# Hybrid stick-breaking and HGRN2 layer: the HGRN2 output projection in pairs of panels by seven products

## What is computed

```
h    = rmsnorm(x, norm_g);  proj = h @ w_in          # 10240 columns
sb_q, sb_k, sb_v, sb_z, hg_q, hg_f, hg_i, hg_z, gate_logits = split(proj)
sb_o = stick_breaking_attention(sb_q, sb_k, sb_v)     # 8 heads of 128
u_sb = (sb_o * silu(sb_z)) @ w_sb_proj                # 1024 x 1024
hg_o = rmsnorm(hgrn2(silu(hg_q), 1 - f, log f, hg_i)) # 8 heads of 128
u_hg = (hg_o * silu(hg_z)) @ w_hg_proj                # 1024 x 1024
y    = sigmoid(gate_sb) * u_sb + sigmoid(gate_hg) * u_hg
out  = rmsnorm(x + y @ w_out, final_norm_g)
```

## Time and profile before

| | |
|---|---|
| median of 3 timed runs | 1359.74 us (1359.3 to 1360.8) |
| the profiled execution | 1358.94 us, its span 1357.2 us |
| mean granted clock of TensorE | 0.997 of full |
| PE busy | 1329.0 us (98%) |
| DVE, ACT, POOL busy | 903.1, 549.4, 709.5 us |
| sb and hg panels on PE | 1087 to 1263 us |
| output product on PE | 1263 to 1351 us |

### The profile page before, as it was taken

The page is one execution under the profiler, slowest core; times in us unless marked ns, Lnnn a source line. Parts: engine busy times, 40 slices in busy tenths (PEclk is TensorE's granted clock), DMA queues, the critical chain, the costliest instruction groups (busy, mean ns, idle before and its releaser), DMA issues.

```text
span 1357.2 us, 22985 instructions
## 1 busy us (share of the span) xinstructions
PE 1329.0 (98%) x8393; PEld 1108.9 (82%) x8393; DVE 903.1 (67%) x1076; ACT 549.4 (40%) x899; POOL 709.5 (52%) x475
## 2 busy tenths in 40 slices
PE   8899999999999999999999999999999999999998
PEld 6788788788878878878888887887887888888886
DVE  5838877877877887787687788778635455645223
ACT  7543355255345335524534533552444431111121
POOL 5655564654665556455466556645578722223310
PEclk9999999999999999999999999999999999999999
DMA  5122111211112211121111211113543485434502
GB/s 187 31 62 65 47 62 32 82 58 46 62 46 73 66 32 62 31 92 56 37 62 46 77 62 31 62 31 118 176 180 133 155 266 191 124 93 132 202 27 98
DMA packets 128168, 118.55 MB, mean 87 GB/s; under 512 B 3920, under 2 KB 110464, under 8 KB 128128
## 3 DMA queue, kind: packets, MB, share of 16 engines
q1 hardware_dynamic: 118816, 92.81, 21.5%
q10 hardware_dynamic: 9312, 25.19, 5.4%
HBM read 88.63 MB, written 29.36 MB: 87 GB/s over the span
## 4 chain that ended last, share of the span: by engine, by line
PE 82%; DVE 7%; issue 5%; POOL 2%; ACT 2%; DMA 1%; ACTq 0%; DVEq 0%; SPq 0%; POOLq 0%
PE banks L1693 44%; PE banks L1986 13%; PE banks L2030 7%; PE banks L1773 5%; PE banks L1751 4%; PE banks L1763 2%; DVE hk L1176 2%; DVE forget L1176 2%; DVE scT L1422 1%; PE banks L1832 1%; PE banks L1737 1%; PE banks L1807 1%; POOL b_lo L631 1%; POOL b_sum L631 1%; PE banks L1834 1%
## 5 line engine op out<-in xcount | busy, mean ns | idle before, releaser
L1693 PE MATMUL banks<-a_hi,b_hi 128*128 128x512 f32 x1064 | 432.7, 407 | 6.4 <-issue 3.8
L1693 PE MATMUL banks<-a_hi,b_lo 128*128 128x512 f32 x1064 | 417.1, 392 | 0.0
L1693 PE MATMUL banks<-a_lo,b_hi 128*128 128x512 f32 x1064 | 415.7, 391 | 0.0
L631 POOL TENSOR_TENSOR b_lo<-w_raw,b_hi 128x512 fp32r<-128x512 f32 x106 | 162.2, 1540 | 231.9 <-ACT b_hi L733 231.9
L631 POOL TENSOR_TENSOR b_lo<-b_sum,b_hi 128x512 fp32r<-128x512 f32 x114 | 167.7, 1471 | 148.2 <-ACT b_hi L733 148.2
L1693 PEld LDWEIGHTS banks<-a_hi,b_hi 128*128 128x128 f32 x1064 | 200.3, 188 | 46.1 <-issue 7.5
L1693 PEld LDWEIGHTS banks<-a_hi,b_lo 128*128 128x128 f32 x1064 | 199.9, 188 | 44.3
L1693 PEld LDWEIGHTS banks<-a_lo,b_hi 128*128 128x128 f32 x1064 | 200.8, 189 | 35.9
L733 ACT ACTIVATE b_hi<-b_sum 128x512 fp32r<-128x512 f32 x114 | 72.0, 632 | 152.5 <-POOL b_sum L631 151.9
L717 POOL TENSOR_TENSOR w_lo<-w_raw,w_hi 128x1024 fp32r<-128x1024 f32 x20 | 54.5, 2730 | 133.5 <-ACT w_hi L733 133.5
L631 POOL TENSOR_TENSOR b_sum<-w_raw 128x512 f32<-128x512 f32 x68 | 102.9, 1513 | 0.0
(11 more groups left out here) (219 smaller groups left out, 2564.8 us busy)
## 6 DMA issues: line engine op xcount, KB each, us to landing
w_raw<-in_w_in SPq DMA_DIRECT2D x72, 512.0 KB, 4.9
gate_d<-gate_out SPq DMA_DIRECT2D x16, 512.0 KB, 4.6
gate_in<-gate_d ACTq DMA_DIRECT2D x32, 256.0 KB, 2.7
x_tok<-in_x SPq DMA_DIRECT2D x8, 512.0 KB, 6.6
z_d<-z_out SPq DMA_DIRECT2D x8, 512.0 KB, 2.7
hz_d<-z_out SPq DMA_DIRECT2D x8, 512.0 KB, 2.7
osb_d<-o_sb SPq DMA_DIRECT2D x8, 512.0 KB, 5.7
ohg_d<-hq SPq DMA_DIRECT2D x8, 512.0 KB, 2.7
```

Of the source, the lines that this page charges most:

```text
L631: return nc.gpsimd.tensor_tensor(dst, a, b, op)
L1693: last = mm(bank, w[:, s, k, :], t[s][:, k, :], start=opens and k == 0 and z == 0, stop=k == QUAD - 1 and z == 2, skip_group_check=not opens)
```

## The change

1. **hg's branch** is made of four pairs by seven products, 12 matmuls each, like the input projection: 336 matmuls for 384. Its weights go through `hg_prepare` (POOL), `hg_split` (ACT) and buffers of their own; only `w_raw` holds raw weights, no second buffer.
2. **The hg operand** is now needed as seven block sums. DVE gates two tiles per sb panel (`gate_ohg`), makes four sums of 2048 elements a partition (`branch_sums`) in panels 5 and 6, and seven low parts (`branch_low`) from panel 6 into the first pair; ACT makes seven high parts of 2048 (`branch_high`).
3. **y's first share** (gated u_sb) is stored to memory by SP (`store_y`) and read back (`load_y`). DVE takes a block in PSUM: add, times gate, plus y's share (`y_part`), ACT makes the high part (`y_high`), DVE the low part (`y_low`).
4. **The output's weights**: panels 0 and 1 are loaded when the last pair's raw weights are free, 2 and 3 behind them, 4 to 7 after the last product.
5. **`HG_AT`**: the pieces from level 6 on come one half product later.
6. **s_ready**: at pair 2 PE waits product by product (P6 and P7 for two operands, P5 for three, P3 for four); ACT's second sigmoid of head 0 waits for all four.
7. In the gate pairs with two or more sb tiles DVE takes c22 ahead of the second `osb_gate`; their low parts come later.

```diff
-HG_AT = {1: 0, 3: 1, 6: 3, 9: 4, 12: 5, 14: 6, 17: 7, 19: 8, 21: 9, 23: 11, 26: 12}
+HG_AT = {1: 0, 3: 1, 6: 3, 9: 4, 12: 5, 15: 6, 18: 7, 20: 8, 22: 9, 24: 11, 27: 12}
+Y_BLOCKS = ((1, 1), (0, 0), (1, 0), (0, 1))
...
+        def hg_freed(engine, n, s):
+            if n > N_PAIRS:
+                engine.wait_ge(product_done, products_before(n - 1, s))
+            elif s in (P5, P2):
+                engine.wait_ge(panel_done, 2 * KT - 2)
+            elif s in (P3, P4):
+                engine.wait_ge(panel_done, 2 * KT)
...
 def load_panel(t, source, first):
+                elif OUT_PANEL0 <= t < OUT_PANEL0 + 2:
+                    sp.wait_ge(raw_sum, 4 * (N_PAIRS + N_HG_PAIRS))
                 else:
                     sp.wait_ge(panel_ready, t - 1)
...
+            def load_hg_pair(n):
+                if n == N_PAIRS:
+                    sp.wait_ge(panel_ready, KT)
+                else:
+                    sp.wait_ge(raw_sum, 4 * n)
+            def load_gate(i):
+                if i < 2:
+                    sp.wait_ge(gated, 2 * KT)
+                else:
+                    sp.wait_ge(y_made, i - 1)
...
+            for i in range(N_HG_PAIRS):
+                if i < N_HG_PAIRS - 1:
+                    load_hg_pair(N_PAIRS + i + 1)
+                else:
+                    load_panel(out_panel(0), w_out[0], 0)
+                    load_panel(out_panel(1), w_out[0], P)
+                    load_y(KT - 1)
+                    load_panel(out_panel(2), w_out[0], 2 * P)
+                    load_panel(out_panel(3), w_out[0], 3 * P)
+                if i == 0:
+                    for e in range(2, KT - 1):
+                        load_y(e)
+                for j in range(4 * i + 2, min(4 * i + 6, 4 * N_HG_PAIRS)):
+                    load_gate(j)
...
+            for i in range(N_HG_PAIRS):                       # DVE
+                n = N_PAIRS + i
+                dve.wait_ge(p1_copied, n + 1)
+                take(n, 0, P6 + 1, hg_u2[:, :], pair_bank(n, P6), hg_u3[:, :])
+                if i == 0:
+                    branch_low(P4)
+                else:
+                    y_low(4 * i - 1)
+                take(n, 1, P7 + 1, hg_u3[:, :], pair_bank(n, P7), hg_u2[:, :])
+                y_part(4 * i, P5, hg_u3)
+                y_part(4 * i + 1, P2, None)
+                y_low(4 * i)
+                y_part(4 * i + 2, P3, hg_u2)
+                y_low(4 * i + 1)
+                y_part(4 * i + 3, P4, hg_u2)
+                y_low(4 * i + 2)
...
 PE:
+                    if isinstance(n, int) and n == 2 and s in SUM_OPERANDS:
+                        pe.wait_ge(s_ready, max(SUM_OPERANDS.index(t) for t in SUM_OPERANDS if t <= s) + 1)
-            pe.wait_ge(s_ready, 4)
             second_half(0)
...
             pe.wait_ge(y_ready, 2 * KT - 1)
+            pe.wait_ge(panel_ready, OUT_PANEL0 + 2)
             for g in range(2):
-                out_group(g, 2, 2)
+                out_group(g, 0, 2)
```

More of the change, by code:

```diff
@@ L389, in build @@
         gated = sem("gated")
-        y_part = sem("y_part")
+        y_stored = [sem("y_stored0"), sem("y_stored1")]
+        y_back = [sem(f"y_back{e}") for e in range(KT)]
+        block_gated = sem("block_gated")
+        y_made = sem("y_made")
         y_hi_ready = sem("y_hi_ready")
@@ L586, in _ @@
+            sp.wait_ge(product_done, PRODUCTS * (N_PAIRS + N_HG_PAIRS))
+            for i in range(NT):
+                sp.dma_start(x_again[i][:, :], x[0, i * P:(i + 1) * P, :]).then_inc(x_again_in, 16)
+            sp.dma_start(fg[:, :], final_g.rearrange("(a n) -> a n", a=1).broadcast_to([P, D])).then_inc(fg_in, 16)
+            for e in range(4, KT):
+                load_panel(out_panel(e), w_out[0], e * P)
             for done, (i, cols) in enumerate(NORM_PIECES):
                 sp.wait_ge(normed, done + 1)
-                sp.dma_start(out[0, i * P:(i + 1) * P, cols], res[:, i, cols]).then_inc(stored, 16)
+                sp.dma_start(out[0, i * P:(i + 1) * P, cols], res[i][:, cols]).then_inc(stored, 16)
@@ L917, in sigmoids @@
                 act.wait_ge(qk_done, 8 * h + j + 1)
+                if isinstance(h, int) and h == 0 and j == 1:
+                    act.wait_ge(s_ready, 4)
                 bank, n_banks, m = score_banks(j)
@@ L1102, in _ @@
                             osb_sigmoid(e)
-                    if p == 7 and not final:
-                        for e in OSB_GATED.get(g, ()):
+                    if p in (7, 10) and not final:
+                        for e in OSB_GATED.get(g, ())[:1] if p == 7 else OSB_GATED.get(g, ())[1:]:
                             osb_high(e)
@@ new lines, in _ @@
+                if t == KT - 2:
+                    for s in (P1, P6, P7):
+                        branch_high(s)
+                if t < KT - 1:
+                    fetch_gate(t + 1)
+            hg_split(N_PAIRS, P1)
+            hg_split(N_PAIRS, P7)
+            branch_high(P5)
+            hg_split(N_PAIRS, P6)
+            hg_split(N_PAIRS, P5)
+            branch_high(P2)
+            hg_split(N_PAIRS, P2)
+            branch_high(P3)
+            for i in range(N_HG_PAIRS):
+                n = N_PAIRS + i
+                last_pair = i == N_HG_PAIRS - 1
+                for p in range(PAIR_POINTS):
+                    if i == 0 and p == 0:
+                        hg_split(n, P3)
+                    if p == 1:
+                        hg_split(n, P4)
+                        act.wait_ge(product_done, PRODUCTS * n + P1 + 1)
+                        act.wait_ge(block_taken, 5 * n - 2)
+                        copy(hg_u3[:, :], pair_bank(n, P1)).then_inc(p1_copied, 1)
+                    if i == 0 and p == 2:
+                        branch_high(P4)
+                    if i > 0 and p == 2:
+                        y_high(4 * i - 1)
+                    following = {6: P1, 7: P7, 9: P6, 10: P5, 11: P2, 12: P3}
+                    if p in following and not last_pair:
+                        hg_split(n + 1, following[p])
+                    if last_pair and p in (4, 5, 8, 12):
+                        e = (4, 5, 8, 12).index(p)
+                        act.wait_ge(product_done, PRODUCTS * n + (P6 if e < 2 else P7) + 1)
+                        split_panel(out_panel(e), out_weights(e)[0])
+                    if p in (10, 11, 13):
+                        y_high(4 * i + (10, 11, 13).index(p))
@@ L1158, in _ @@
+            y_high(4 * N_HG_PAIRS - 1)
+            act.wait_ge(product_done, PRODUCTS * (N_PAIRS + N_HG_PAIRS))
+            for e in range(4, KT):
+                split_panel(out_panel(e), out_weights(e)[0])
             for i in range(NT):
@@ L1654, in _ @@
+            y_low(4 * N_HG_PAIRS - 1)
             dve.wait_ge(x_again_in, 16 * NT)
[L1655 removed]
             def last_norm(i):
```

405 lines of the change are left out of this document (264 added, 141 removed).

## The result

The changed kernel takes 1402.4 us (median of 4 runs, 1399.1 to 1404.2) against 1359.5 for the kernel before: ratio 1.031 (95% interval 1.029 to 1.033), 43 us slower, where 1364 was forecast. PE's busy time moved little; its waits did.

What follows compares the result with a forecast made beforehand. PE was taken as the bound, with matmuls for 98% of the span. Terms −10.9 − 3.8 + 0 + 0.6 + 5.8 + 2.6 + 8.2 + 1.7 = +4.2 gave 1364 us; eight-in-ten range 1353 to 1369.

Steps and rivals of the forecast that it cites:

- Later points: Heads: level 6 later removes the wait for hk, but PE then waits for v_diff; 0 for seven heads.
- v_diff as an anchor: Heads: the norm's chain keeps v_diff at the same absolute time, so PE arrives 1.36 us earlier and waits.
- the later points pay: Rival, heads: v_diff ready earlier, PE keeps 1.3 us in each of seven heads, −9.1, about 1355 us; chance 0.10.
- sb's branch: y's share, gates' loads and x's second reading lie beside PE's products in sb's branch, a few loads; 0.
- hg's pairs: hg's branch: PE stalls of +5.8 in the first pair and +2.6 in the other three.
- The first pair: hg's first pair: PE waits near P2 and P3 for what DVE and ACT make; +5.8 us.
- The others: hg's other pairs: POOL's period 20.5 us against PE's 19.2, 1.3 us lost twice; +2.6, bounds 0 and 2 each.
- Contention: hg's first pair: DVE and POOL lock each other out; at all four overlaps, stall 7.1 and sum +5.5, not +4.2.
- Front: Pair 2: PE waits product by product for low parts, so kappa's transpose comes earlier; −3.8, bounds 0 and −5.5.
- gates: Gate pairs: wait for gate_out goes, but PE waits for POOL; gains 0, +0.6 for later operands and loads.
- tail: Ahead of the output: PE waits +8.2 for panel loads, splits and y's last blocks, then +1.7 at the lower clock.

Runs made afterwards that it cites:

- e1: Changed kernel with the HG_AT table of the kernel before: 1374.2 us, ratio 1.011 to the kernel before.
- e2: Kernel before with the changed kernel's HG_AT table alone: 1388.5 us, ratio 1.021.
- e4: Kernel before with the new HG_AT table, but the output piece back at point 23, ahead of P3: 1373.2 us, ratio 1.010.
- g2: Kernel before with levels 6 and 7 and the transposes at new points, states, output and norm at old ones: 1357.4 us, ratio 0.998.
- e3: Kernel before with level 6 alone one half product later, all later pieces where they were: 1351.6 us, ratio 0.994.
- e6: e5 with DVE taking the first half of sb's panel 1 ahead of its two hg operand tiles: 1363.8 us, ratio 1.003.
- f3: f2 with DVE taking the first half of sb's panels 1 to 4 ahead of the hg operand tiles: 1361.8 us, ratio 1.001.
- f2: e5 with e7's tail order, and hg's two panels loaded with separate semaphores, the second fetched before sum t4: 1357.5 us, ratio 0.999.
- f1: Kernel before with two parts alone, s_ready product by product and level 6 one half product later: 1347.8 us, ratio 0.991.
- e7: e6 with y's last high parts ahead of output panel splits, last gates ahead of panel 3, block 14's low part ahead of block 15: 1360.1 us.
- f4: f3 with the last row of y's share read back ahead of the output's first two panels: 1363.6 us, ratio 1.002.
- e5: Changed kernel with the old HG_AT table except level 6 one half product later: 1362.8 us, ratio 1.003.
- g1: f2 with hg operand tiles taken one in sb's panel 1, two in panels 2 to 4, one in panel 5: 1356.1 us, ratio 0.997.

## Why the prediction was wrong

**Later points: the step that failed.** It said that the pieces "keep their distances" and so stand at the same absolute times, with 0 for seven heads and 0 for the last head's 1.3. Its half about v_diff held in the changed kernel (seven waits, 1.63 us for 1.3, against hk's 1.31 won). What it left out is that the pieces keep their distances from one another but not from P3, which doesn't move. States half a product nearer to P3, the output piece behind it: 2.0 us a head for z_out (14.0), 5.1 for the clock behind it, and in the last head and the gate pairs 5.2 more than forecast (with the old points, e1, this stage is as before). e2 and e4 show it: 29 us for the table alone, 14 with the output piece ahead of P3. Second, it asked of the moved pieces only whether they are late for v_diff, not whether DVE has room for them: g2 shows 5.8 us for level 7 and the transposes alone. Of the 38 us between forecast and result the table is 28 (e1). And the reason given for the 0, v_diff as an anchor, is refuted by e3: with only level 6 moved, v_diff came earlier with PE, and 7.7 us were won. The rival "the later points pay" was right that v_diff is no anchor, for another reason than the one it gave, and for the whole table it had the sign wrong.

**sb's branch: forecast 0, +4.9.** "A few loads of some 4 us" counted each load alone. Together they fill the DMA engines (share 0.96 to 1.06 in three stretches of 10 us from 1120 to 1150). The tiles' loads (z_in) take 7.6 us to landing and the weights 10.8, where they took 5.5 and 6.6 between 1094 and 1128 in the kernel before. DVE, which holds PE's bank, stands behind them, and behind POOL (1.3 us). The waits of 3.2 and a fall of the clock of 1.7 make the 4.9. e6 and f3 show that a new order alone moves the wait; no run shows an edit that takes it away.

**hg's pairs: +8.4 forecast, +13.4.** The first pair had waits of 3.5 us and a clock fall of 1.7 (5.2, forecast 5.8). u2 was there 25.1 us after the start of sb's last panel, inside the forecast's 24.3 to 26.9; but at P3, for which the forecast counted the whole first y_part chain, PE waited only for its first operation, 0.30 us. Without the clock, which the forecast had not charged here, the pair would have been 2.3 us below it. The others had 2.4 and 2.5 (forecast 1.3 each): the load took 5.9 us, not 4.9, and a second fall of the clock (1.7) came with them. The mechanism stands, by f2; the term was too small by the load and by the clock, which the prediction charged only ahead of the output. The two terms make 11.9; another 1.5 us of the stage lie in smaller gaps.

**Contention.** In the first pair POOL took 3.22 us for a sum and 6.28 for two low parts, in place of 1.30 and 2.56, while DVE's operations of 2048 elements ran (2.39 to 3.36 us). Two of these rows of the kernel after, POOL's and DVE's:

```profile
1207.79 6.28 POOL L748 TENSOR_TENSOR hg_b_lo<-w_raw,hg_b_hi 128x512 fp32r<-128x512 f32 x2 [0.32 <-ACT hg_b_hi L877]
1209.56 3.36 DVE L1377 TENSOR_TENSOR og_lo<-og_raw,og_hi 128x2048 fp32r<-128x2048 f32 x1
```

That is 5.6 us more on POOL in three operations, where the forecast had 2.04 for each. The Trainium skill ("SBUF — State Buffer", section "Who interferes with whom") says that such a pair of engines blocks one another for whole instructions; the durations agree. The delay reached PE through t4 and ACT's queue, as the rows of the first pair show, yet the stall was smaller than the 7.1 us worked out from it. No run took the contention away, so what it cost PE is not shown.

**Front, gates, tail.** The front gave 4.3 at kappa, for 3.8, and f1 holds its gain (3.8 under e3); in the eleven kernels with this front kappa's transpose starts between 72.4 and 73.9. With the old points the gate stage differs from before by 0.2 us, for +0.6. The tail's stage was +10.1 for +9.9, and that so near is luck, for errors cancel: the wait was 7.0 for 8.2, and what lies behind it, nearly all the slower clock, 3.1 for 1.7. In the wait too. The forecast's terms add up to 19.1 us and not 19.5, and the chain from the end of t4 (1279.43) to the output took 20.4, with 5.2 us to ACT's first split for a load of 3.7. But t4 ended 13.2 us ahead of PE's end, not 11.3, since the clock behind PE's wait at P6 had put that end off by 1.7. e7 shows that the order on ACT, SP and DVE made 2.6 us of the wait. The rest is loads behind t4, the share and the gates, and f4 shows that exchanging two of them doesn't help.

**What is left of the change.** With a good table (e5) it stands 3 us above the kernel before, and some 15 above f1, which has the same table and front but keeps the old branch. The 48 matmuls are worth 10.9 us, and stalls, clock and tail took them back more than twice over. The best version of the new branch tried, g1, is still 8 us above f1. Whether more buffers for the raw weights would turn that was not tried.

## What to carry to other kernels

When pieces are moved along a row of products, hold each piece against every wait that doesn't move with it, the release of a bank above all: distances among the moved pieces say nothing of it. Move one piece at a time: one entry of this table won 7.7 us, all six lost 29. A branch with fewer matmuls but one buffer, a sum ahead of the reload and a dependent chain at its end needs its stalls priced with the clock behind each, and its loads at the latency they have together.

## What the runs showed of the hardware

- The granted clock fell to the lower level (0.5) behind most of PE's waits of 2.5 us or more, and behind some of 2.0: three of seven alike in the changed kernel, four of seven in e2. A fall cost 1.7 us, behind the longest waits up to some 3. Waits of 1.63 us in seven heads were never followed by a fall.
- Loads of weights of 512 KB took 4.9 us median in hg's branch and 10.8 in the densest stretch of sb's (311 to 386 GB/s there).
- DVE's product of two operands in SBUF (1024 elements) took 2.52 us beside POOL's low part and 1.23 without it; POOL's sum (512) took 3.22 beside DVE's low part of 2048 elements and 1.29 without it.
